# mLSTM decode state: sample-query products alternate between two column groups of PSUM, with a per-head add of the two partial sums

## The chip, the cores and the metric

The program runs on one core of one Trainium2 chip. The metric is the device time of one execution in microseconds (us); lower is better. The tensor engine (PE) multiplies a stationary operand, loaded into its array first, with a moving operand that streams through it, and writes to PSUM: 128 partitions, 8 banks of 512 fp32 columns each. VectorE (DVE), ScalarE (ACT), GpSimd (POOL) and the DMA queue fed by SyncE (SP) run beside it and are synchronised by semaphores.

## The reference, cut to what matters

One inference step of a two-layer model for a prompt of 256 tokens and 8 samples of 4 new tokens (32 sample tokens). The part that the change touches is the mLSTM of layer 1: 4 heads of width 512, each sample with an old state C0 of 512x512 per head.

```python
num = jnp.einsum('btsh,bshe->bthe', w_intra, vc) + w_inter[..., None] * jnp.einsum('bthd,bhde->bthe', qc, C)
den = jnp.sum(w_intra, axis=2) + w_inter * jnp.einsum('bthd,bhd->bth', qc, n)
h = num / jnp.maximum(jnp.abs(den), jnp.exp(-m_t))[..., None]
C_new = decay[..., None, None] * C + jnp.einsum('bshd,bshe->bhde', kw, vc)
```

For the samples, the second term of `num` is the product of each sample's 4 scaled queries with its own old state, and `C_new` is the decayed old state plus an outer product of the sample's keys and values. All of it is in fp32.

## The kernel before, in words

The kernel is one hand-ordered program per engine. The dense matrices are streamed as weights through two buffers of 2 MB; that part (lines 1582 to 1584 on PE) is not touched. The mLSTM stage stands between the dense steps IN_C and OUT_C, and during it the weight buffers serve as a ring of 8 slots (`cring`), each holding half of one sample's state for one head: 2 tiles of 128x512.

Loops: for each head h of 4, for each sample b of 8, for each half of the state. A state tile index e runs over 4, two to a half.

- PE, `old_state(h, b, half)` (line 1914): for its two tiles, a matmul with the scaled queries of sample b as the stationary operand (128 rows, 32 columns, zero outside the sample's own 4 columns) and the state tile as the moving operand, 512 columns wide. All 32 such products of a head, and one product of the head's own 32 tokens (line 1941), add up in `ps[0:NS, 2, :]`, that is partitions 0 to 31 of bank 2. An fp32 matmul of the program appears in the trace as two weight loads and two matmul passes.
- PE, `outer(h, b, half)` (line 1930): two matmuls of 96x128 by 96x512 (fp32r, one pass each) into banks 0 and 1. It waits for `c_new`: the two banks are used by every half, so the DVE must have taken the half before.
- DVE, `new_state(h, b, half)` (line 1385): two `scalar_tensor_tensor` of 128x512 that read banks 0 and 1 and update the slot; then SP stores the slot (line 558) and loads the one six items ahead (line 549).
- `chunk(h, b)`: other work of the head and of the next one, spread over b on all engines. PE: denominators and numerators at b=0, key sums at b=1, the prompt's own state (`outer(h, NB, half)`, line 1933) at b=2 and 3, next head's projections at b=4, 5 and 6, its rows and scores at b=7. The last head has nothing of the next head to do at b=4 to 7.

PE's order for one sample before is: `old_state` half 0, `outer` half 0, `old_state` half 1, `outer` half 1, `chunk`.

At the end of a head (`chunk`, b=7), ACT copies the sum out of PSUM into `hs[:, h]` (line 931), squares it (line 934) and, if there is a next head, runs its exponentials (lines 891 to 893). DVE writes `y1_lo` (line 1430) and then makes the next head's queries (`queries`, lines 1335 to 1345) and score weights (`weights`, lines 1360 and 1361). After the last head, DVE scales `hs` (lines 1450 to 1459), PE transposes it (line 1983), DVE combines it (lines 1463 to 1467), and only then do the steps of OUT_C start.

The column group of a 32-column product follows from its PSUM partitions. Elsewhere in the kernel, `sample_scores(b)` (lines 1667 and 1669, layer 0) writes sample b's attention scores to the 32 partitions `32*(b % 4)`, so its column group changes at each new b; 1667 writes two wide passes into each of two banks, 1669 a narrow product of the own keys.

Of the kernel before, what the change touches and what calls it, by code (L numbers as in the profile page):

```python
# [21 lines left out]
ALU = mybir.AluOpType  # L22
ACT = mybir.ActivationFunctionType
AX = mybir.AxisListType

P = 128
D = 1024
SEQ = 256
NB = 8
# [96 lines left out]
def program(nc, A, O):  # L126
    ctx = ExitStack()
    with ctx:
# [187 lines left out]
        def sem(name):  # L316
            sems[name] = ctx.enter_context(nc.semaphore(name))
            return sems[name]
# [103 lines left out]
        h_ready = sem("h_ready")  # L422
        h_sq = sem("h_sq")
        hs_psum = sem("hs_psum")
        hs_taken = sem("hs_taken")
        hs_sq = sem("hs_sq")
        hs_mean = sem("hs_mean")
# [35 lines left out]
        def item(h, b, half):  # L463
            return ITEMS * h + ORDER.index((b, half))

        def loads(i):

            return sum(1 for j in range(i % C_SLOTS, i + 1, C_SLOTS) if ORDER[j % ITEMS][0] < NB)
# [125 lines left out]
        def _(act):  # L594
# [310 lines left out]
            def chunk(h, b):  # L905
                if b == 0:
                    act.wait_ge(den_psum, h + 1)
                    act.activation(stok[:, 0, h:h + 1], ps[0:NS, 3, SEQ:SEQ + 1], ACT.Abs)
                    act.activation(dn, ps[:, 3, 0:SEQ], ACT.Abs).then_inc(den_abs, 1)
                if b == 1:  # L910
                    act.wait_ge(h_ready, h + 1)
                    act.activation(qf[:, :, 0:SEQ], hT, ACT.Square).then_inc(h_sq, 1)
                if b == 3:
                    act.activation(dn, staged(h, "mean")[:, 0:SEQ], ACT.Sqrt, bias=tiny[:, 0:1], scale=1.0 / DH
                                   ).then_inc(stage_read_a, 1)
                if b == 4 and h + 1 < NH:
                    qk(h + 1)
                if b == 5 and h + 1 < NH:
                    keys_by_token(h + 1)
                    own_keys(h + 1)  # L920
                if b == 6:
                    if h + 1 < NH:
                        values_by_token(h + 1)
                    act.wait_ge(y1_full, h + 1)
                    act.activation(y1_hi[:, ET * h:ET * h + ET, 0:SEQ], hT, ACT.Copy).then_inc(y1_hi_ready, 1)
                if b == 7:
                    if h + 1 < NH:
                        head_rows(h + 1)

                    act.wait_ge(hs_psum, h + 1)  # L930
                    act.activation(hs[:, h], ps[0:NS, 2, :], ACT.Copy).then_inc(hs_taken, 1)
                    act.wait_ge(hs_taken, h + 1)

                    act.activation(fold[0:NS].rearrange("p a b -> p (a b)")[:, 0:DH], hs[:, h], ACT.Square, accum_out=stok[:, 1, h:h + 1]).then_inc(hs_sq, 1)
                    if h + 1 < NH:
                        exps(h + 1)
# [29 lines left out]
        def _(dve):  # L966
# [428 lines left out]
            def chunk(h, b):  # L1395
                if b == 0:

                    dve.wait_ge(den_abs, h + 1)
                    order.after(dve.tensor_tensor(dn, dn, bc[:, h % 2, R_EN:R_EN + SEQ], ALU.max))
                    order.after(dve.reciprocal(dn, dn))  # L1400
                    dve.wait_ge(num_psum, h + 1)
                    dve.tensor_tensor(hT, ps[:, 4:6, :].rearrange("p a (c t) -> p (a c) t", t=SEQ),
                                      dn.unsqueeze(1).to_broadcast([P, ET, SEQ]), ALU.mult).then_inc(h_ready, 1)
                if b == 1:
                    new_n(h)
                if b == 2:
                    new_state(h, NB, 0)
                if b == 3:
                    new_state(h, NB, 1)
                if b == 4:  # L1410
                    dve.wait_ge(stage_read_a, reads(use(h, "mean"))[1])
                    order.after(dve.reciprocal(dn, dn))
                    for e in range(ET):
                        order.mark(dve.scalar_tensor_tensor(hT[:, e], hT[:, e], pcol("norm_w", ET * h + e), dn,
                                                            ALU.mult, ALU.mult))
                if b == 5:
                    order.wait()
                    for e in range(ET):
                        m = ET * h + e
                        order.mark(dve.scalar_tensor_tensor(hT[:, e], xcc[:, m, 0:SEQ], pcol("skip", m), hT[:, e],  # L1420
                                                            ALU.mult, ALU.add))
                    if h + 1 < NH:
                        keys_low(h + 1)
                    order.wait()
                    dve.tensor_tensor(hT, hT, z[:, ET * h:ET * h + ET, 0:SEQ], ALU.mult).then_inc(y1_full, 1)
                if b == 6 and h + 1 < NH:
                    values_low(h + 1)
                if b == 7:
                    dve.wait_ge(y1_hi_ready, h + 1)
                    dve.tensor_tensor(y1_lo[:, ET * h:ET * h + ET, 0:SEQ], hT, y1_hi[:, ET * h:ET * h + ET, 0:SEQ],  # L1430
                                      ALU.subtract).then_inc(y1_ready, 1)
                    if h + 1 < NH:
                        queries(h + 1)
                        arguments(h + 1)
                        weights(h + 1)
# [134 lines left out]
        def _(pe):  # L1570
# [330 lines left out]
                    last = pe.matmul(out[:, c0:c0 + NB], kst[:, h % 2, es], seln, start=True, stop=True)  # L1901
                last.then_inc(stage_full, 1)

            def old_state(h, b, half):

                i = item(h, b, half)
                s = i % C_SLOTS
                if h and b == half == 0:
                    pe.wait_ge(hs_taken, h)
                pe.wait_ge(qs_ready, h + 1)  # L1910
                pe.wait_ge(c_in[s], 16 * loads(i))
                for d in range(HD2):
                    e = HD2 * half + d
                    last = pe.matmul(ps[0:NS, 2, :], qz_of1(h, e, b), cring[:, s, d], start=b == e == 0,  # L1914
                                     stop=b == NB - 1 and e == ET - 1, skip_group_check=True)
                return last

            def outer(h, b, half):
# [17 lines left out]
            def chunk(h, b):  # L1936
                if b == 0:
                    denominators(h)
                    numerators(h)

                    pe.matmul(ps[0:NS, 2, :], ew[0:NS, 3 * P:3 * P + NS], vtk_s, start=False, stop=False,
                              skip_group_check=True)
                if b == 1:
                    key_sums(h)
# [23 lines left out]
            scores(0)  # L1968
            for h in range(NH):
                for b in range(NB):  # L1970
                    for half in range(2):
                        last = old_state(h, b, half)
                        if b == NB - 1 and half == 1:
                            last.then_inc(hs_psum, 1)
                        outer(h, b, half)
                    chunk(h, b)

# [133 lines left out]
```

## Time and profile before

| | us |
|---|---|
| median of 3 runs | 1517.96 |
| lowest, highest | 1515.53, 1520.9 |
| span of the profiled execution | 1518.3 |
| mLSTM stage in it (first `old_state` to last `outer`) | 922.25 to 1209.06 |

The profile gives the span of the profiled execution; it stands 0.3 us above the median. In its rows, PE is a matmul pass and PEld a weight load; a timeline row gives start, duration and the instructions merged into it, and in brackets the engine's idle time before it with what ended it. "x4" on line 1914 is two matmuls of the program. Matmul ends are modelled, so starts are the firmer number.

### The profile page before, as it was taken

The page shows a single profiled execution, that of the slowest core. Times are in us where ns is not written, and L with a number is a line of the kernel's source. Part 1 is how long each engine was busy: PE and PEld are TensorE (multiplying, and loading weights), DVE is VectorE, ACT ScalarE, POOL GpSimd, SP SyncE. Part 2 cuts the span into 40 slices and gives each one's busy share as a digit, 9 for nine tenths or more (in the row PEclk, how much of TensorE's full clock was granted, in tenths as well). Part 3 has the DMA queues.
Part 4 walks back from the last instruction along what each step waited for, and adds up shares of the span by engine and source line. Part 5 has one row for each costly group of instructions (what it writes and reads, how often), then busy time and mean ns, then how long its engine had stood idle before and what let it go on. Part 6 is the DMA issues. An engine that isn't in the chain of part 4 may idle for free.

```text
span 1518.3 us, 21716 instructions
## 1 busy us (share of the span) xinstructions
PE 1372.2 (90%) x8383; PEld 1101.8 (73%) x8383; DVE 705.4 (46%) x1032; ACT 526.1 (35%) x846; POOL 155.3 (10%) x244
## 2 busy tenths in 40 slices
PE   4999799879999799999799979999999787999995
PEld 4999233369989699999699945444444286999995
DVE  5545624521113654434657434555555645544343
ACT  5333022411113465433435243232332143555341
POOL 2000000000000222100360031010000002222000
PEclk9999699969989799999799799999999988999998
DMA  7444278738744154444244013767676853444340
GB/s 261 165 161 160 100 255 264 244 124 254 243 141 160 56 174 166 159 167 166 70 171 161 26 58 124 254 228 260 214 267 210 272 201 111 152 162 160 137 166 31
DMA packets 68587, 260.25 MB, mean 171 GB/s; under 512 B 7780, under 2 KB 9124, under 8 KB 60584
## 3 DMA queue, kind: packets, MB, share of 16 engines
q1 hardware_dynamic: 68520, 259.32, 49.2%
q8 instruction: 46, 0.75, 0.2%
q14 instruction: 21, 0.17, 0.0%
HBM read 217.57 MB, written 41.73 MB: 171 GB/s over the span
## 4 chain that ended last, share of the span: by engine, by line
PE 85%; DVE 8%; ACT 3%; issue 2%; DMA 2%; POOL 1%; SPq 0%; POOLq 0%; DVEq 0%; ACTq 0%
PE ps L1582 17%; PE ps L1584 16%; PE ps L1583 16%; PE ps L1914 7%; PE ps L1723 7%; PE ps L1667 4%; PE ps L1930 3%; PE ps L1933 2%; DVE x L1024 1%; PE ps L1819 1%; PE ps L1811 1%; PE ps L1624 1%; DMA kv<-in_kv 1%; PE ps L1643 1%; DVE cring L1385 1%
## 5 line engine op out<-in xcount | busy, mean ns | idle before, releaser
L1582 PE MATMUL ps<-xin_hi,w_hi 128*128 128x288 f32 x1088 | 335.6, 308 | 51.3 <-DVE xin_lo L1003 29.4
L973 DVE TENSOR_TENSOR w_lo<-w_raw,w_hi 128x1024 fp32r<-128x1024 f32 x232 | 282.8, 1222 | 199.7 <-ACT w_hi L605 199.3
L1583 PE MATMUL ps<-xin_lo,w_hi 128*128 128x288 f32 x1088 | 328.9, 302 | 0.0
L1584 PE MATMUL ps<-xin_hi,w_lo 128*128 128x288 f32 x1088 | 327.6, 301 | 0.0
L605 ACT ACTIVATE w_hi<-w_raw 128x1024 fp32r<-128x1024 f32 x232 | 243.0, 1055 | 236.0 <-PE ps L1584 223.2
L1582 PEld LDWEIGHTS ps<-xin_hi,w_hi 128*128 128x128 f32 x1088 | 211.2, 194 | 59.7 <-issue 40.5
L1583 PEld LDWEIGHTS ps<-xin_lo,w_hi 128*128 128x128 f32 x1088 | 212.5, 195 | 0.5
L1584 PEld LDWEIGHTS ps<-xin_hi,w_lo 128*128 128x128 f32 x1088 | 212.6, 195 | 0.0
L1582 PE MATMUL ps<-hid_hi,w_hi 128*128 128x288 f32 x512 | 153.1, 299 | 5.7 <-POOL hid_lo L1504 5.7
L1583 PE MATMUL ps<-hid_lo,w_hi 128*128 128x288 f32 x512 | 152.4, 298 | 0.0
L1584 PE MATMUL ps<-hid_hi,w_lo 128*128 128x288 f32 x512 | 152.0, 297 | 0.0
L1385 DVE SCALAR_TENSOR_TENSOR cring<-cring,bc,ps 128x512 f32<-128x512 f32 x128 | 90.0, 745 | 83.0 <-PE ps L1930 82.9
L1914 PE MATMUL ps<-cring,qz 128*32 128x512 f32 x256 | 121.8, 598 | 0.0
L1667 PE MATMUL ps<-kv,qz 128*32 128x448 f32 x256 | 103.5, 549 | 6.3 <-issue 4.3
L1723 PE MATMUL ps<-kv,pT 128*32 128x128 f32 x896 | 103.0, 277 | 0.0
L1723 PEld LDWEIGHTS ps<-kv,pT 128*32 128x32 f32 x896 | 98.0, 112 | 6.1 <-issue 5.3
L1582 PEld LDWEIGHTS ps<-hid_hi,w_hi 128*128 128x128 f32 x512 | 97.4, 190 | 6.1 <-issue 6.1
L1584 PEld LDWEIGHTS ps<-hid_hi,w_lo 128*128 128x128 f32 x512 | 97.7, 191 | 0.0
L1583 PEld LDWEIGHTS ps<-hid_lo,w_hi 128*128 128x128 f32 x512 | 97.4, 190 | 0.0
L1035 DVE SCALAR_TENSOR_TENSOR relu<-ps,rstd 128x288 f32<-128x288 f32 x64 | 29.3, 457 | 93.1 <-PE ps L1584 93.0
L1914 PEld LDWEIGHTS ps<-cring,qz 128*32 128x32 f32 x256 | 22.9, 109 | 63.5 <-issue 62.5
L1504 POOL TENSOR_TENSOR hid_lo<-relu,hid_hi 128x288 f32 x64 | 52.2, 815 | 156.3 <-ACT hid_hi L673 156.3
(343 smaller groups left out, 1680.8 us busy)
## 6 DMA issues: line engine op xcount, KB each, us to landing
w_raw<-in_weights SPq DMA_DIRECT2D x58, 2048.0 KB, 8.1
kv<-in_kv SPq DMA_DIRECT2D x128, 448.0 KB, 4.2
cring<-in_C SPq DMA_DIRECT2D x64, 512.0 KB, 4.8
out_Cs<-cring SPq DMA_DIRECT2D x64, 512.0 KB, 3.7
out_Cp<-cring SPq DMA_DIRECT2D x8, 512.0 KB, 3.0
x<-in_x SPq DMA_DIRECT2D x1, 1152.0 KB, 5.2
out_v<-gaqkv SPq DMA_DIRECT2D x1, 1152.0 KB, 4.2
out_k<-gaqkv SPq DMA_DIRECT2D x1, 1152.0 KB
```

Source lines behind the costliest of these rows:

```text
L605: act.activation(w_hi[:, l % UM], w_raw[:, u % 2, l % UM], ACT.Copy).then_inc(hi_ready, 1)
L973: dve.tensor_tensor(w_lo[:, l % UM], w_raw[:, u % 2, l % UM], w_hi[:, l % UM], ALU.subtract).then_inc(lo_ready, 1)
L1385: last = dve.scalar_tensor_tensor(cring[:, s, e], cring[:, s, e], bc[:, h % 2, R_DECAY + b:R_DECAY + b + 1], ps[:, e, :], ALU.mult, ALU.add)
L1504: pool.tensor_tensor(hid_lo[:, bass.ds(m, 1)].rearrange("p a t -> p (a t)"), relu2[:, l], hid_hi[:, bass.ds(m, 1)].rearrange("p a t -> p ( ...
L1582: pe.matmul(ps[:, j, 0:T], w_hi[:, j, ws], hi, start=start and kk == 0, stop=False)
L1583: pe.matmul(ps[:, j, 0:T], w_hi[:, j, ws], lo, start=False, stop=False)
L1584: last = pe.matmul(ps[:, j, 0:T], w_lo[:, j, ws], hi, start=False, stop=stop and kk == UK - 1)
L1667: pe.matmul(ps[part, 2 * f + c, 0:NK // 2], lhs, kv[:, s, c * NK // 2:(c + 1) * NK // 2], start=h == 0, stop=h == H - 1, skip_group_check= ...
L1723: last = pe.matmul(out, pT[:, kt, c0:c0 + 32], kv[:, s, P * kt:P * kt + P], start=False, stop=kt == KT - 1, skip_group_check=True)
L1914: last = pe.matmul(ps[0:NS, 2, :], qz_of1(h, e, b), cring[:, s, d], start=b == e == 0, stop=b == NB - 1 and e == ET - 1, skip_group_check= ...
L1930: last = pe.matmul(ps[:, d, :], kst[:, h % 2, es], vb[:, (NB * h + b) % 2], start=True, stop=True)
L1933: last = pe.matmul(ps[:, d, :], ktok[:, tt, es], vw[:, tt], start=tt == 0, stop=tt == 1)
```

## The change

Three things change together.

1. `old_state(h, b)` now does all four tiles of a sample in one run, ahead of both `outer` halves; it waits for both halves of the state to be loaded. PE's order for one sample becomes: `old_state` (4 matmuls), `outer` half 0, `outer` half 1, `chunk`.
2. Tile e goes to the group of 32 partitions `g = 2*(h % 2) + e % 2` of the same bank 2. Within a head the products alternate between two groups; even heads use partitions 0 to 63, odd heads 64 to 127. The head's own product goes to the first of the two. With two heads' sums apart, the wait for `hs_taken` reaches back two heads instead of one.
3. The two partial sums are added per head: ACT copies one (`hs_half`), DVE adds the other from PSUM to it (`hs_taken`), and ACT's square waits for that. The DVE instruction stands between `y1_lo` and the next head's queries.

```diff
@@ ACT, chunk b=7
                     act.wait_ge(hs_psum, h + 1)
-                    act.activation(hs[:, h], ps[0:NS, 2, :], ACT.Copy).then_inc(hs_taken, 1)
+                    g = NS * 2 * (h % 2)
+                    act.activation(hs[:, h], ps[g + NS:g + 2 * NS, 2, :], ACT.Copy).then_inc(hs_half, 1)
                     act.wait_ge(hs_taken, h + 1)
@@ DVE, chunk b=7
                                       ALU.subtract).then_inc(y1_ready, 1)
+                    g = NS * 2 * (h % 2)
+                    dve.wait_ge(hs_half, h + 1)
+                    dve.tensor_tensor(hs[:, h], ps[g:g + NS, 2, :], hs[:, h], ALU.add).then_inc(hs_taken, 1)
                     if h + 1 < NH:
                         queries(h + 1)
@@ PE
-            def old_state(h, b, half):
-
-                i = item(h, b, half)
-                s = i % C_SLOTS
-                if h and b == half == 0:
-                    pe.wait_ge(hs_taken, h)
+            def old_state(h, b):
+
+                if h >= 2 and b == 0:
+                    pe.wait_ge(hs_taken, h - 1)
                 pe.wait_ge(qs_ready, h + 1)
-                pe.wait_ge(c_in[s], 16 * loads(i))
-                for d in range(HD2):
-                    e = HD2 * half + d
-                    last = pe.matmul(ps[0:NS, 2, :], qz_of1(h, e, b), cring[:, s, d], start=b == e == 0,
-                                     stop=b == NB - 1 and e == ET - 1, skip_group_check=True)
+                for half in range(2):
+                    i = item(h, b, half)
+                    pe.wait_ge(c_in[i % C_SLOTS], 16 * loads(i))
+                for e in range(ET):
+                    g = 2 * (h % 2) + e % 2
+                    s = item(h, b, e // HD2) % C_SLOTS
+                    last = pe.matmul(ps[NS * g:NS * g + NS, 2, :], qz_of1(h, e, b), cring[:, s, e % HD2],
+                                     start=b == 0 and e < 2, stop=b == NB - 1 and e >= 2, skip_group_check=True)
                 return last
@@ PE, the loop
                 for b in range(NB):
+                    last = old_state(h, b)
+                    if b == NB - 1:
+                        last.then_inc(hs_psum, 1)
                     for half in range(2):
-                        last = old_state(h, b, half)
-                        if b == NB - 1 and half == 1:
-                            last.then_inc(hs_psum, 1)
                         outer(h, b, half)
                     chunk(h, b)
```

PE's order, last head, samples 4 and 5 (`c_in` is the load of a ring slot, `c_new` the DVE's update of the half before). Before:

```order
L1914 MATMUL ps<-cring,qz_149 32x512 [waits c_in2,qs_ready]
L1914 MATMUL ps<-cring,qz_149 32x512
L1930 MATMUL ps<-vb,kst 128x512 [waits vb_ready,stage_read_v,c_new]
L1930 MATMUL ps<-vb,kst 128x512
L1914 MATMUL ps<-cring,qz_149 32x512 [waits c_in3,qs_ready]
L1914 MATMUL ps<-cring,qz_149 32x512
L1930 MATMUL ps<-vb,kst 128x512 [waits vb_ready,stage_read_v,c_new]
L1930 MATMUL ps<-vb,kst 128x512
```

And now:

```order
L1920 MATMUL ps<-cring,qz_149 32x512 [waits c_in3,c_in2,qs_ready]
L1920 MATMUL ps<-cring,qz_149 32x512 x3
L1936 MATMUL ps<-vb,kst 128x512 [waits vb_ready,stage_read_v,c_new]
L1936 MATMUL ps<-vb,kst 128x512
L1936 MATMUL ps<-vb,kst 128x512 [waits vb_ready,stage_read_v,c_new]
L1936 MATMUL ps<-vb,kst 128x512
```

The two runs of two query products became one run of four, and nothing stands any more between the two outer products, the second of which waits for the DVE.

DVE's order at the end of the last head (`stok` are the per-token factors of the sample outputs). Before:

```order
L1385 SCALAR_TENSOR_TENSOR cring<-cring,bc,ps 128x512 [waits c_in7,c_mm]
L1385 SCALAR_TENSOR_TENSOR cring<-cring,bc,ps 128x512
L1430 TENSOR_TENSOR y_lo<-hT,y_hi 128x4x256 [waits y1_hi_ready]
L1450 TENSOR_TENSOR stok<-stok,tokg_s 32x4
L1451 RECIPROCAL stok<-stok 32x4 [waits v_order]
L1453 TENSOR_TENSOR stok<-stok 32x4 [waits hs_sq,v_order]
```

And now:

```order
L1387 SCALAR_TENSOR_TENSOR cring<-cring,bc,ps 128x512 [waits c_in7,c_mm]
L1387 SCALAR_TENSOR_TENSOR cring<-cring,bc,ps 128x512
L1432 TENSOR_TENSOR y_lo<-hT,y_hi 128x4x256 [waits y1_hi_ready]
L1436 TENSOR_TENSOR hs<-ps,hs 32x512 [waits hs_half]
L1455 TENSOR_TENSOR stok<-stok,tokg_s 32x4
L1456 RECIPROCAL stok<-stok 32x4 [waits v_order]
L1458 TENSOR_TENSOR stok<-stok 32x4 [waits hs_sq,v_order]
```

The add came in behind `y_lo`, and the wait for `hs_sq` (ACT's square) now hangs on it.

## Rows read from the trace of the kernel before

**Rows 1.** Engines in a stretch: from:to, length, busy (count) of each, PEclk, DMA share, GB/s.

```profile
922.00:1210.80 288.80, 268.82 (x973) 119.43 (x972) 156.23 (x268) 76.67 (x137) 4.34 (x12) 1.00 0.70 236
```

**Rows 2.** Timeline, head 2, sample 1: start us, us, engine, line.

```profile
1081.69 1.90 PE L1914 MATMUL ps<-cring,qz 128*32 128x512 f32 x4
...
1083.52 0.73 PE L1930 MATMUL ps<-vb,kst 96*128 96x512 f32 x2
...
1084.19 1.90 PE L1914 MATMUL ps<-cring,qz 128*32 128x512 f32 x4
1084.30 1.41 DVE L1385 SCALAR_TENSOR_TENSOR cring<-cring,bc,ps 128x512 f32<-128x512 f32 x2 [2.18 <-PE ps L1930]
...
1086.02 0.30 PEld L1930 LDWEIGHTS ps<-vb,kst 96*128 96x128 f32 x2 [0.84 <-DVE cring L1385]
```

**Rows 3.** Timeline, last head, sample 5, PE alone.

```profile
1196.94 0.73 PE L1930 MATMUL ps<-vb,kst 96*128 96x512 f32 x2 [1.85 <-DVE cring L1385]
```

**Rows 4.** Timeline, last head, samples 5 and 6, DVE alone.

```profile
1195.48 1.40 DVE L1385 SCALAR_TENSOR_TENSOR cring<-cring,bc,ps 128x512 f32<-128x512 f32 x2
1197.71 1.41 DVE L1385 SCALAR_TENSOR_TENSOR cring<-cring,bc,ps 128x512 f32<-128x512 f32 x2 [0.83 <-PE ps L1930]
...
1201.88 1.40 DVE L1385 SCALAR_TENSOR_TENSOR cring<-cring,bc,ps 128x512 f32<-128x512 f32 x2
```

**Rows 5.** Timeline, head 0, sample 6: DVE, then PE's loads.

```profile
981.66 1.41 DVE L1385 SCALAR_TENSOR_TENSOR cring<-cring,bc,ps 128x512 f32<-128x512 f32 x2
...
983.13 0.30 PEld L1930 LDWEIGHTS ps<-vb,kst 96*128 96x128 f32 x2 [0.84 <-DVE cring L1385]
```

**Rows 6.** Timeline of PE's matmuls: within sample 2 of `sample_scores`; from sample 3 to 4.

```profile
222.85 0.92 PE L1667 MATMUL ps<-kv,qz 128*32 128x448 f32 x2
...
236.77 0.75 PE L1667 MATMUL ps<-kv,qz 128*32 128x448 f32 x2
...
237.15 0.22 PE L1669 MATMUL ps<-gaqkv,qz 128*32 128x32 f32 x2
```

**Rows 7.** Timeline of PE's weight loads, `sample_scores`, from sample 3 to 4.

```profile
236.95 0.14 PEld L1667 LDWEIGHTS ps<-kv,qz 128*32 128x32 f32 x2
237.15 0.11 PEld L1669 LDWEIGHTS ps<-gaqkv,qz 128*32 128x32 f32 x1
```

**Rows 8.** View of line 1328: ns min/median/max, first and last start, forms.

```profile
L1328 DVE TENSOR_TENSOR vst<-ps,vst x4: 683/683/683, 916.4 to 1137.8; 32x512 fp32r<-32x512 f32 x4
```

**Rows 9.** Timeline, from head 1 to head 2.

```profile
1070.49 0.29 DVE L1345 TENSOR_TENSOR qn<-qn,par 128x128 f32<-128x128 f32 x1
...
1071.76 0.14 PEld L1914 LDWEIGHTS ps<-cring,qz 128*32 128x32 f32 x2
...
1072.96 0.17 DVE L1361 TENSOR_TENSOR ew<-ew,ps 32x32 f32<-32x32 f32 x1
...
1074.37 1.40 DVE L1385 SCALAR_TENSOR_TENSOR cring<-cring,bc,ps 128x512 f32<-128x512 f32 x2 [1.25 <-PE ps L1930]
```

**Rows 10.** Timeline, end of the stage and start of OUT_C.

```profile
1209.05 0.63 ACT L934 ACTIVATE fold<-hs 32x512 f32<-32x512 f32 x1
...
1209.59 0.18 ACT L934 ACTIVATION_READ_ACCUMULATOR fold<-hs 32x1 f32 x1
...
1211.55 0.14 DVE L1450 TENSOR_TENSOR stok<-stok,tokg_s 32x4 f32<-32x4 f32 x1
...
1211.93 0.15 DVE L1453 TENSOR_TENSOR stok<-stok 32x4 f32<-32x4 f32 x1
...
1220.90 0.60 PE L1582 MATMUL ps<-y_hi,w_hi 128*128 128x288 f32 x1 [5.39 <-DVE y_lo L1472]
```

**Rows 11.** Engines in stretches, columns as in the first group.

```profile
626.20:629.10 2.90, 0.06 (x2) 0.06 (x1) 0.84 (x2) 2.25 (x4) 0.80 (x1) 1.00 0.00 0
...
630.60:633.80 3.20, 3.20 (x16) 3.20 (x15) 0.48 (x1) 0.00 (x0) 0.00 (x0) 0.50 0.54 113
...
1192.00:1204.00 12.00, 8.82 (x23) 2.27 (x21) 10.38 (x17) 1.78 (x2) 0.00 (x0) 1.00 0.64 225
```

More of the change, by code:

```diff
@@ L424, in program @@
         hs_psum = sem("hs_psum")
+        hs_half = sem("hs_half")
         hs_taken = sem("hs_taken")
@@ L1939, in chunk @@
                     numerators(h)
-                    pe.matmul(ps[0:NS, 2, :], ew[0:NS, 3 * P:3 * P + NS], vtk_s, start=False, stop=False,
+                    g = NS * 2 * (h % 2)
+                    pe.matmul(ps[g:g + NS, 2, :], ew[0:NS, 3 * P:3 * P + NS], vtk_s, start=False, stop=False,
                               skip_group_check=True)
```

## Prediction

> **What bounds the kernel now.** I read the stretches first, to find which part of the span the change touches, then the timeline of the mLSTM stage, then the places where its pattern breaks. Everything outside the stage from 922 to 1221 us keeps its instructions, so the sum is made over this stage. In it the tensor clock is granted in full and PE shows 268.82 of 288.80 us busy [rows 1], but a busy PE says little here: the modelled ends of four query passes cover their own draining. The timeline says more. For one half of a state, the query products start at 1081.69, the outer products at 1083.52 (1.83 us later), the next query products at 1084.19 (0.67 later), and the next outer products at 1086.02 (1.83 later) [rows 2]. So a half takes 2.50 us from outer product to outer product. The DVE starts on the two banks 0.78 us after the outer products begin and needs 1.41 us, until 1085.71, while PE comes for the banks at 1086.02 [rows 2]: between two halves of one sample PE is last by 0.31 us, though the bracket names the DVE. This pattern, 2.50 us from half 0 to half 1, stands in 27 of the 32 sample steps (4 heads by 8 samples).
>
> It breaks in five. In samples 5 and 6 of the last head the DVE, busy with the head's output, comes late: PE stood idle 1.85 us for it [rows 3]. There DVE ends at 1196.88 (1195.48 + 1.40) and PE goes on at 1196.94, 0.06 us later, and the DVE starts again 0.77 us after that, at 1197.71 [rows 3, 4]. In sample 6 of heads 0 to 2 the DVE is the limit too: it ends at 983.07 and the outer products follow at 983.13 [rows 5].
>
> **The change part by part.**
>
> *Between the halves.* Nothing stands any more between the two outer products of a sample, so the second follows the first as fast as the DVE lets it: 0.77 us until the DVE starts, 1.41 us of DVE, 0.06 us until PE goes on [rows 2 to 4], 2.24 us in place of 2.50. That is 0.26 us less in each of the 27 steps. In the other five the DVE already set the time and its own chain doesn't shrink: nothing. The total for this part is 27 x 0.26 = 7.0 us less. The price of the part is cover: the 1.90 us of query products that ran beside the DVE in this gap [rows 2] now run ahead of the first outer products, where the next paragraph counts them.
>
> *The run of four query products.* It lies on PE's path from one sample to the next. Before, half of it did: 1.83 us from its first pass to the outer products, four passes 0.43 us apart (a matmul of the program is two passes; 1.90 us for four, of which the last takes some 0.6 us to its modelled end, leaves 1.3 us for three steps) [rows 2]. Now it is eight passes, A A B B A A B B in program order, where A and B are the two column groups. Does the array run A and B side by side? The trace of before doesn't show this run, but it shows a change of column group in `sample_scores`. Two wide passes of one group take 0.92 us together, so the second starts 0.38 after the first [rows 6]. At the change from partitions 96 to 127 to partitions 0 to 31, two wide passes take 0.75 us together, from 236.77 [rows 6]: the new group's pass starts some 0.21 us after the old group's wide pass, inside it. And the old group's two narrow passes, which come earlier in the program, start at 237.15, 0.38 us after their own group's last pass [rows 6]: neither stream slowed the other. Even the order is not kept: the new group's weights are loaded at 236.95, ahead of the old group's at 237.15 [rows 7]. So a pass that waits for its own group lets one of the other group by. If that holds in the run, A and B go side by side with four steps as before, B behind A by the time in which its two predecessors are loaded, some 0.03 us each (two loads merge into 0.14 us where one takes 0.11 [rows 7]). I take 1.89 us for the whole run, 0.06 more than 1.83. This estimate's bounds are 1.83 (no lag) and 1.83 + 4 x 0.43 = 3.55 (no overlap at all). I take the lower end because the row at 236.77 is the same kind of pass, fp32 with 32 columns, and I keep the other for the rivals; one difference is that there the two groups wrote to different banks, and here both write to bank 2. Cost: 27 x 0.06 = 1.6 us. In sample 6 of heads 0 to 2 the DVE hides it (it starts 0.26 us later than PE's outer products would allow), and in samples 5 and 6 of the last head it stands behind the wait of 1.85 us [rows 3].
>
> One page weighs against this. The Trainium skill, TensorE: Matmul & The Clock Gate, section "Part 3: Packing small matmuls — row/col tiling", says that matmuls of different tiles overlap, but start and end strictly in program order. By that rule the run would take five steps, the sum would be the first rival's, and the rows at 236.95 and 237.15 disagree with it.
>
> *The add, heads 0 to 2.* DVE gets one instruction of 32x512 with a PSUM operand; line 1328 has that shape and takes 0.68 us [rows 8]. It stands ahead of the next head's queries, which end at 1070.78 where PE first loads them at 1071.76 [rows 9]: 0.98 us of slack for 0.68. Behind ACT's wait for the add are the square, the load of the exponential table, the exponentials, and the copy for sample 1; the DVE's `weights` end at 1073.13 and its next work starts at 1074.37 [rows 9], 1.24 us of slack for a shift of at most 0.9. So I cost these three at nothing. Were the cover gone, they would cost 0.7 to 0.9 each, 2 to 3 us.
>
> *The add, last head.* Here nothing hides it. Before, ACT's square was done at 1209.77, long before DVE came to line 1453 at 1211.93 [rows 10]. Now the add starts where line 1450 did, at 1211.55, ends at 1212.23, the square and its read-out take 0.72 us (1209.05 to 1209.77) [rows 10], and with 0.05 us for two semaphores line 1453 starts at about 1213.0: 1.1 us later. OUT_C starts on the DVE's last piece of this chain [rows 10], so all of it counts.
>
> *Waits that move.* Both halves of a state must have landed before its first product. PE waited for no load in the stage, and loads are issued six items ahead, three samples of 5 us at least. No cost. The wait for `hs_taken` goes back a head; it wasn't late before. No gain. Drains of the array between 32-column and 128-column work are halved in number, but those that go were beside the DVE's work and are in the 2.24 us.
>
> *The clock.* PE will be idle about 1.5 us in each step, as it is today at b=2 and 3, with a full clock. But in sample 5 of the last head the gap of 1.85 us grows by the 1.9 us of products that move out of it, to some 3.7 us, and in sample 6 to 3.2. Such a gap was followed by a lower clock elsewhere: PE did almost nothing from 626.20 to 629.10 and ran at 0.50, the 1.2 GHz level, from 630.60 to 633.80 [rows 11]; in 1192 to 1204 it is 1.00 today [rows 11]. Three microseconds at half rate slow a run of four steps by 1.7 us. If they fall on sample 6 the DVE hides most of it, if on sample 7 nothing does. Bounds 0 and about 4 us (two such runs and their outer products); I take 0.5.
>
> *Sum.* -7.0 + 1.6 + 0 + 1.1 + 0.5 = -3.8 us. The profiled span is 1518.3, the median 1518.0, so the two stand for each other: 1518.0 - 3.8 = 1514.2 us.
>
> **The rivals.**
>
> *Strict order (slower).* If a pass can't go ahead of one that waits, A A B B A A B B overlaps only where the group changes: A2 with B1, B2 with A1 and so on. Eight passes then take five steps in place of four: 0.43 us more per run, against 0.26 gained between the halves. Both count in 30 steps now, since the DVE has no slack left in those three of [rows 5] either: 30 x 0.17 = 5.1, plus 1.1 and 0.5, gives 6.7 us more, 1524.7 us. It decides against the change once the run takes more than about 2.0 us (0.26 less the 1.6 us of the ends spread over 27 steps is 0.2 us above 1.83). For it: program order is the simple case. Against it: rows 6 and 7. Chance 10%.
>
> *No overlap in one bank.* If two groups that write to the same bank take turns, the change doesn't do what it says: eight steps, 1.71 us more per run, less 0.26, in 30 steps 43.5, plus 1.6: 45 us more, 1563 us. For it: no row shows two groups in one bank. Against it: a product of full width writes all 128 partitions of one bank at once. Chance 7%.
>
> *The clock falls in earnest.* The 4 us above in place of 0.5: 1517.7 us, which is no change. Chance 10%.
>
> *More than reckoned.* No lag in the run and no clock loss: -7.0 + 1.1 = -5.9, 1512.1 us. It is the near end of my own case.
>
> **How the numbers follow.** My case has 73%, the other three 27%. A measurement of this kernel can tell about 0.3%, 4.6 us, from no change. My case lies between 1512 and 1516, and three runs of one kernel lay 5 us apart, so it falls on both sides of 1513.4: I put 40 of its 73 below (faster) and 33 above (no change). No change gets the clock's 10 less 2 for a worse end, 41 in all. Slower gets 10 + 7 + 2 = 19. The range takes in my case with the spread of the runs and strict order: 1509 to 1525.
>
> **What would show it.** In the trace of after: from the first query pass to the outer products 1.9 us (2.3 for strict order, 3.5 for none); passes of a run starting in pairs 0.06 us apart; 2.24 us between the two outer products; the add of 0.68 us at four places with PE's first product of a head not waiting for it; 1.1 us more from the last update of the state to OUT_C; PEclk of the last head's stretch. I am wrong if the run takes over 2.0 us, if the second outer products come later than 2.3 us after the first, or if a wait for a load or for the queries appears in front of the run.

## The result: 2.6% slower, and the profile after

| | kernel before | kernel after |
|---|---|---|
| median of 4 runs | 1516.74 us (1513.92 to 1520.9) | 1556.26 us (1552.38 to 1560.01) |
| ratio to before, 95% interval | 1 | 1.0256 (1.0226 to 1.0286) |
| span of the profiled execution | 1518.3 us | 1551.2 us |
| stage, first query product to last outer product | 286.4 us | 321.1 us |
| granted clock over the stage | 1.00 | 0.85 |

The forecast was 1514.2 us, and its range ended at 1525. The profiled execution of after is 32.9 us longer, and the stage alone is 34.7 us longer, so what happened, happened there.

The stage as a whole and four stretches of head 2 (columns as in [rows 1]: from:to, length, busy and count of PE, PEld, DVE, ACT, POOL, then PEclk, DMA share, GB/s):

```profile
919.10:1240.20 321.10, 255.61 (x968) 130.57 (x967) 156.62 (x268) 75.22 (x133) 4.33 (x12) 0.85 0.62 210
1093.60:1097.00 3.40, 3.40 (x13) 2.96 (x12) 2.18 (x2) 0.75 (x2) 0.00 (x0) 0.50 0.72 222
1097.00:1103.80 6.80, 5.30 (x25) 2.30 (x23) 2.93 (x4) 1.30 (x2) 0.00 (x0) 1.00 0.16 60
1103.90:1110.60 6.70, 6.70 (x25) 3.68 (x24) 1.45 (x5) 0.38 (x1) 0.00 (x0) 0.50 0.68 219
1110.70:1114.00 3.30, 1.36 (x4) 0.49 (x4) 1.81 (x3) 0.34 (x1) 0.00 (x0) 1.00 0.09 35
```

Before, PEclk was 1.00 here and PE modelled as busy for 268.82 of 288.80 us [rows 1]; now PE is busy 255.61 of 321.10 us and the clock swings between its two levels, 2.4 GHz (1.00) and 1.2 GHz (0.50). The trace has 20 pieces at 0.50 in this stage. The page shows the same in its row of granted clocks over 40 slices of the span, where the stage lies in slices 24 to 32:

```profile
PEclk9999699889989799999897978879797879899998
```

The timeline of PE over one step at full clock and the next one mostly at half clock (start, length, engine, line, operation, count of passes, in brackets the idle time ahead and what ended it; a program's matmul is two passes):

```profile
1098.66 1.91 PE L1920 MATMUL ps<-cring,qz 128*32 128x512 f32 x8
1100.50 0.73 PE L1936 MATMUL ps<-vb,kst 96*128 96x512 f32 x2
1102.73 0.73 PE L1936 MATMUL ps<-vb,kst 96*128 96x512 f32 x2 [1.50 <-DVE cring L1387]
...
1107.01 3.63 PE L1920 MATMUL ps<-cring,qz 128*32 128x512 f32 x8
1110.57 0.76 PE L1936 MATMUL ps<-vb,kst 96*128 96x512 f32 x2
1112.83 0.73 PE L1936 MATMUL ps<-vb,kst 96*128 96x512 f32 x2 [1.50 <-DVE cring L1387]
```

At full clock all is as the sum had it: eight passes at L1920 are through in 1100.50 - 1098.66 = 1.84 us, no more than four of them took before (1.83) [rows 2], and the second outer products follow the first after 1102.73 - 1100.50 = 2.23 us. At half clock the same run takes 1110.57 - 1107.01 = 3.56 us. Nothing but the clock differs between the two.

That the two column groups really run side by side shows in the weight loads, same step, PEld:

```profile
1098.65 0.14 PEld L1920 LDWEIGHTS ps<-cring,qz 128*32 128x32 f32 x4 [0.84 <-issue]
...
1099.11 0.12 PEld L1920 LDWEIGHTS ps<-cring,qz 128*32 128x32 f32 x2 [0.31 <-issue]
...
1099.54 0.12 PEld L1920 LDWEIGHTS ps<-cring,qz 128*32 128x32 f32 x2 [0.31 <-issue]
```

The eight loads come as four, two and two, 0.43 to 0.46 us apart. With all products in one group (e1_one_group below) they come as two and then six single ones, 0.43 us apart. The rows don't name the group; that a bunch of two is one load for each group is read from the program's order.

The view of waits for PE, over the stage (engine, line, waited for: us in total, times, longest). After:

```profile
PE ps L1936 <- DVE cring L1387: 50.9, 32, 3.7
PE ps L1939 <- DVE cring L1387: 12.0, 8, 1.5
```

and before, the same two places:

```profile
PE ps L1933 <- DVE cring L1385: 12.0, 8, 1.5
PE ps L1930 <- DVE cring L1385: 3.2, 2, 1.9
```

PE stood idle beside the DVE in 2 of 32 steps before; now it does in all 32, for 50.9 us in all. The page gives the query products 121.8 us busy before and 68.9 now. So two things were taken out of the stage together: the work that covered the DVE, and about half of the time in which PE streams query products.

### The profile page after: what moved, and what is told of

Read it like the earlier page. It is cut to its first block, busy times and chain, and to the rows that moved or that the text cites. A ratio compares the mean times of both kernels' runs of the same rounds, so it can differ in the third digit from the quotient of the medians.

```text
span 1551.2 us, 21690 instructions
## 1 busy us (share of the span) xinstructions
PE 1355.2 (87%) x8383; PEld 1107.9 (71%) x8383; DVE 708.2 (46%) x1036; ACT 526.5 (34%) x846; POOL 154.9 (10%) x244
## 4 chain that ended last, share of the span: by engine, by line
PE 81%; DVE 9%; ACT 3%; issue 3%; DMA 2%; POOL 1%; SPq 0%; POOLq 0%; DVEq 0%; ACTq 0%
PE ps L1587 16%; PE ps L1589 16%; PE ps L1588 16%; PE ps L1728 6%; PE ps L1672 4%; PE ps L1920 4%; PE ps L1939 3%; PE ps L1936 3%; DVE cring L1387 2%; PE ps L1824 1%; PE ps L1864 1%; DMA kv<-in_kv 1%; DVE x L1026 1%; PE ps L1816 1%; PE ps L1629 1%
## 5 line engine op out<-in xcount | busy, mean ns | idle before, releaser
L1936 PE MATMUL ps<-vb,kst 96*128 96x512 f32 x128 | 48.5, 461 | 50.9 <-DVE cring L1387 50.9
L1936 PEld LDWEIGHTS ps<-vb,kst 96*128 96x128 f32 x128 | 19.7, 194 | 96.1 <-DVE cring L1387 67.1
L1920 PE MATMUL ps<-cring,qz 128*32 128x512 f32 x256 | 68.9, 663 | 0.0
```

Source lines behind the costliest of these rows:

```text
L1920: last = pe.matmul(ps[NS * g:NS * g + NS, 2, :], qz_of1(h, e, b), cring[:, s, e % HD2], start=b == 0 and e < 2, stop=b == NB - 1 and e >= ...
L1936: last = pe.matmul(ps[:, d, :], kst[:, h % 2, es], vb[:, (NB * h + b) % 2], start=True, stop=True)
```

## Experiments

The two clock levels say what the time went on, not why the level fell. A prediction that counts on "1.5 us idle is harmless" needs to know. The theories:

- **A, share of work**: the clock falls when PE streams for too little of the time, by whatever cause. The change took both 1.5 us of cover in each step and some 50 us of streaming out.
- **B, the hole**: the idle 1.5 us between the two outer products in each step does it.
- **C, two streams at once**: two column groups running together do it.
- **D, both**: holes and thinned-out passes each take from the clock, and add up. It is A with the holes and the passes told apart.
- **E, thrown-away work doesn't count**: fill matmuls wouldn't hold the clock, so a kernel with fills tells nothing.

Time at half clock is worked out from the windows: 2 x (1 - PEclk) x length, so 2 x 0.15 x 321.1 = 96 us for after. PEclk has two digits, so these figures are good to some 3 us. Stage and PEclk are those of the one profiled execution. The mean clock over the whole execution is known of every run, and it was 0.904 to 0.908 in the four of after and 0.934 to 0.944 in those of before. The first four experiments were timed beside the same runs of before (median 1517.01 us of 8), the last four beside others (1518.35 us of 19). The ratio is taken from the runs round by round, so it can differ from the quotient of the medians, by 0.2% for e3_split and 0.3% for e4_half_products.

| kernel | median us | ratio, 95% | stage us | PEclk | at half clock, us |
|---|---|---|---|---|---|
| after | 1556.26 | 1.0256 (1.0226 to 1.0286) | 321.1 | 0.85 | 96 |
| e1_one_group | 1597.8 | 1.0521 (1.0497 to 1.0546) | 368.2 | 0.89 | 81 |
| e2_fill | 1527.14 | 1.0061 (1.0038 to 1.0084) | 293.9 | 0.94 | 35 |
| e3_split | 1507.25 | 0.9916 (0.9885 to 0.9946) | 278.5 | 0.90 | 56 |
| e4_half_products | 1507.59 | 0.991 (0.9879 to 0.994) | 278.6 | 0.89 | 61 |
| e5_split_fill | 1498.91 | 0.9875 (0.9847 to 0.9904) | 266.6 | 0.97 | 16 |
| e6_fill4 | 1519.67 | 1.0005 (0.9989 to 1.0021) | 288.5 | 0.99 | 6 |
| e7_after_all_filled | 1518.51 | 0.9999 (0.9979 to 1.0019) | 291.7 | 0.95 | 29 |
| e8_split_fill_some | 1502.78 | 0.9899 (0.9877 to 0.9922) | 269.1 | 0.95 | 27 |

### e1_one_group: the new order without the second column group

```
-                    g = 2 * (h % 2) + e % 2
+                    g = 2 * (h % 2)
```

(ACT copies that one group, the DVE's add becomes an operation of the same size on `hs` alone, and the `start` and `stop` flags follow the one sum.)

> The order of the changed kernel (four products in one run, then both outer products), but all products in one group of 32 partitions; the DVE instruction stays as an in-place maximum of hs with itself, so the per-head chain is as long. Theory A (the tensor clock falls because the engine streams for too small a part of the time, overlapped products counting once): nothing overlaps, the engine streams as long as before, the granted clock stays at 1.00 in the mLSTM stage, the run takes 3.55 us, time about 1517 + 44 = 1561 us. Theory B (it falls because of the hole of 1.5 us between the two outer products of every step): the hole is there, the clock falls as in the changed kernel, 1580 us or more. Theory C (it falls because two groups stream at once): clock stays, 1561 us.

Measured: 1597.8 us. Window of the stage, and one step of PE's timeline at full clock:

```profile
917.10:1285.30 368.20, 305.14 (x968) 143.90 (x965) 156.31 (x268) 75.66 (x135) 4.32 (x12) 0.89 0.55 185
```

```profile
966.97 3.62 PE L1920 MATMUL ps<-cring,qz 128*32 128x512 f32 x8
970.52 0.73 PE L1936 MATMUL ps<-vb,kst 96*128 96x512 f32 x2
972.75 0.73 PE L1936 MATMUL ps<-vb,kst 96*128 96x512 f32 x2 [1.50 <-DVE cring L1387]
```

With one group the eight passes take 970.52 - 966.97 = 3.55 us at full clock, so the second group is worth 3.55 - 1.84 = 1.71 us a step: this is what the change was to bring, and it does. The clock falls without any overlap too (0.89), so the overlap isn't needed for a fall, and C alone can't carry the result. B had 1580 us or more. PE is modelled as busy for 305.14 of 368.20 us, 83%, against 80% in after: the hole of 1.50 us is the same in both. That is what B says; but after has 15 us more at half clock in a stage 47 us shorter, so the hole isn't all of it. A had 1561 us and a clock of 1.00 for this kernel and missed by 37 us: it had reckoned with as much streaming as before, but not with the longer step, of which that is a smaller share.

### e2_fill: a matmul without use in the hole

```
                     outer(h, b, 0)
+                    fill(h, 1)
                     outer(h, b, 1)
```

`fill` multiplies `ones` by `par[:, 0:512]` into 32 partitions of the other head's group in bank 2; nobody reads it.

> The changed kernel plus one fp32 matmul of 128x32 by 128x512 (two passes) between the two outer products of each step, into the two-group area of the other head that nobody reads; its result is thrown away. It should end 1.65 us after the first outer product starts, before the DVE is done at 2.24, and cost nothing in itself. Theory A: the clock stays at 1.00 for most of the stage, time 1512 to 1525 us. Theory B: the hole is filled, the same. Theory C: the clock falls as before or more, 1550 us or more.

Measured: 1527.14 us, 29 us less than after, by adding work, and 2 us above the range that A and B had for it. The hole, in PE's timeline (fill, then the second outer products):

```profile
963.65 1.04 PE L1946 MATMUL ps<-par,ones 128*32 128x512 f32 x2
...
965.23 0.73 PE L1936 MATMUL ps<-vb,kst 96*128 96x512 f32 x2 [0.53 <-DVE cring L1387]
```

```profile
918.30:1212.20 293.90, 258.71 (x1036) 118.56 (x1033) 156.33 (x268) 76.10 (x135) 4.33 (x12) 0.94 0.68 230
```

Two passes of 0.43 us turn a hole of 1.50 us into one of 0.53, and the time at half clock falls from 96 to 35 us. E is refuted: useless streaming holds the clock. It also shows that the slow time in after is the clock's, since no wait, no load and no dependence has been taken out.

### e3_split: two column groups in the old order

```
+            def old_state(h, b, half):
...
+                for d in range(HD2):
+                    e = HD2 * half + d
+                    g = 2 * (h % 2) + d % 2
```

The query products of each half stand ahead of that half's outer products again, as before; each half's two products go to the two groups.

> Two groups, but the order of the kernel before (products of half 0, outer product 0, products of half 1, outer product 1). Each half's two products overlap: 0.98 us from their start to the outer product in place of 1.83, so a step loses 0.26 between the halves and 0.85 ahead of the first: 30 x 0.85 + 27 x 0.26 = 32 us at full clock, 1486 us. The hole beside the DVE is 0.6 us. Theory A: streaming time per step is as small as in the changed kernel and the step shorter; the clock falls in parts of the stage, some 15 to 30 us are lost of the 32: 1500 to 1520 us. Theory B: no long hole, clock 1.00, 1486 us. Theory C: clock falls as in the changed kernel, 1515 us or more.

Measured: 1507.25 us, ratio 0.9916, faster than both kernels. One step of PE's timeline, in sample 6, and the stage:

```profile
973.68 1.05 PE L1920 MATMUL ps<-cring,qz 128*32 128x512 f32 x4
974.66 0.73 PE L1936 MATMUL ps<-vb,kst 96*128 96x512 f32 x2
975.32 1.05 PE L1920 MATMUL ps<-cring,qz 128*32 128x512 f32 x4
978.00 0.73 PE L1936 MATMUL ps<-vb,kst 96*128 96x512 f32 x2 [1.63 <-DVE cring L1387]
```

```profile
922.30:1200.80 278.50, 240.17 (x971) 115.26 (x969) 156.23 (x268) 75.99 (x135) 4.33 (x12) 0.90 0.72 243
```

Four passes now take 974.66 - 973.68 = 0.98 us where they took 1.83 [rows 2]. The second products stand beside the DVE, so most steps have a hole of some 0.5 us only (this one, where the DVE's other work comes between, has 1.63); the clock is still 0.90, where B had 1.00 and 1486 us. So the hole of 1.5 us in every step isn't needed for a fall. But not all holes are small here. The view of waits for PE over the stage has the eight at b = 2 and 3 as before, and one of 3.0 us:

```profile
PE ps L1936 <- DVE cring L1387: 22.1, 29, 3.0
PE ps L1939 <- DVE cring L1387: 12.0, 8, 1.5
```

e8_split_fill_some below takes the long ones out. The gain expected at full clock was some 6 us too high as well, an estimate: the stage of e5_split_fill, 266.6 us with 16 of them at half clock, would be some 260 at full clock, and the expectation had 286.4 - 32 = 254. In samples 3, 6 and 7 of heads 0 to 2 the DVE is last, not PE, and what PE saves there is waited away.

### e4_half_products: half of the products, one group

```
-                for d in range(HD2):
+                for d in range(1):
```

This is an edit of before, and the `stop` flag follows it. It leaves out half of the samples' old-state products.

> The kernel before with one of the two query products of each half left out (half of the old-state products of the samples are missing from the output). The engine's timetable is that of e3_split, with no two passes at once. Theory A: the same time and clock as e3_split. Theory B and theory C: clock 1.00, 1485 us; if e3_split is slower than this one at a lower clock, two streams at once cost clock by themselves.

Measured: 1507.59 us, ratio 0.991.

```profile
965.61 0.72 PE L1930 MATMUL ps<-vb,kst 96*128 96x512 f32 x2 [0.52 <-DVE cring L1385]
...
968.96 1.04 PE L1914 MATMUL ps<-cring,qz 128*32 128x512 f32 x2
969.94 0.73 PE L1930 MATMUL ps<-vb,kst 96*128 96x512 f32 x2
970.60 1.04 PE L1914 MATMUL ps<-cring,qz 128*32 128x512 f32 x2
```

```profile
917.70:1196.30 278.60, 241.19 (x843) 116.15 (x840) 154.49 (x265) 75.54 (x135) 4.34 (x12) 0.89 0.72 243
```

This is the cleanest pair of the study. e3_split runs four passes in two streams, e4_half_products two passes in one stream; on PE's time line they take the same 1.0 us, and the two kernels agree in time (1507.25 and 1507.59), stage (278.5 and 278.6) and clock (0.90 and 0.89; over whole executions 0.916 to 0.927 and 0.919 to 0.929). The overlap as such costs nothing that these runs can tell, which spread over 10 us each: C is refuted as the cause of the loss. What counts is for how long PE streams, not how much it does meanwhile.

### e6_fill4: four passes of fill in the hole

`fill(h, 2)` in place of `fill(h, 1)` of e2_fill.

> The changed kernel with two thrown-away matmuls (four passes) between the outer products of each step, as many as the kernel before has of real ones there. The step between the halves goes back to 2.50 us. Theory D: apart from the last head's two waits the engine streams at least as long as before; clock 1.00 nearly everywhere, 1518 to 1522 us. Theory E: 1550 us or more.

Measured: 1519.67 us, ratio 1.0005.

```profile
1063.99 1.91 PE L1920 MATMUL ps<-cring,qz 128*32 128x512 f32 x8
1065.83 0.73 PE L1936 MATMUL ps<-vb,kst 96*128 96x512 f32 x2
1066.49 1.90 PE L1946 MATMUL ps<-par,ones 128*32 128x512 f32 x4
1068.33 0.73 PE L1936 MATMUL ps<-vb,kst 96*128 96x512 f32 x2
```

```profile
922.50:1211.00 288.50, 271.60 (x1097) 120.36 (x1095) 156.32 (x268) 75.26 (x133) 4.34 (x12) 0.99 0.69 234
```

Here everything of the change is in place, and PE's occupation is about what it was before (271.60 of 288.50 us here, 268.82 of 288.80 in [rows 1]): four passes ahead of the second outer products (1068.33 - 1065.83 = 2.50 us, the old distance [rows 2]) and a run of 1.84 us ahead of the first. Time and clock are those of before within the spread (0.99 and 1.00, some 6 us at half clock). The eight holes of 1.5 us at b = 2 and 3 are still there, 12.0 us in all, and one of 1.9 us. So the groups, the run of eight, the added operation on the DVE and the moved waits together cost nothing that the times can tell (the operation's 1.3 us at the end, below, is within the spread); what after lost hangs on what stood in the hole.

### e7_after_all_filled: every hole of after filled, none lengthened

After each first outer product a fill of 512 and one of 192 columns (in samples 5 and 6 of the last head four and three of 512, where the hole is longer); the same before the outer products of `NB` at b = 2 and 3.

> The changed kernel with all its waits filled as in e5_split_fill. Theory D: the clock holds, and the sum of the prediction without its clock term is met: 1517 - 4.3 = 1513 us. Theory E: 1550 us or more.

Measured: 1518.51 us, ratio 0.9999. That is 38 us less than after and some 5 us above the 1513 expected.

```profile
916.80:1208.50 291.70, 280.17 (x1135) 129.21 (x1133) 156.35 (x268) 76.08 (x135) 4.33 (x12) 0.95 0.68 232
```

29 us at half clock remained, though PE is modelled as busy for 280.17 of 291.70 us (96%). In before it was 93% [rows 1] with a clock of 1.00. So the busy share of the profile is not what the clock follows. The remaining falls come back at like places of heads 0 to 2 (at 986.9, 1065.4 and 1140.5 us, and again some 20 us later). What PE does ahead of those places is the small matmuls of the key sums and of a head's end, but no run took these alone. e6_fill4 has the same matmuls there and no fall. It has more idle time, 13.9 us of waits for the DVE against 8.4 here, but four passes of 512 columns as fill in each step, where this kernel has two of 512 and two of 192. So idle time alone doesn't order the two. What differs between them is the thinner fill, and the filled holes at b = 2 and 3 and in the last head; no run changed the fill by itself, and why the falls come at just these places stays open.

### e5_split_fill and e8_split_fill_some: how much the clock still holds in the split order

e5_split_fill is e3_split with fills of 512 and 192 columns ahead of each second outer product and of the outer products of `NB`; e8_split_fill_some keeps only those at b = 2 and 3 and in the last head:

```
                         last = old_state(h, b, half)
...
+                        if half and h == NH - 1 and b in (5, 6):
+                            fill(h, *((512,) * (4 if b == 5 else 3)))
                         outer(h, b, half)
```

> e3_split with thrown-away matmuls (128x32 by up to 512 columns, the other head's groups of bank 2) in every place where the tensor engine waits for the DVE: 512 and 192 columns beside the second half's products of each step and ahead of the prompt state's outer products at b=2 and 3, four and three of 512 in samples 5 and 6 of the last head. They fit in the waits by the rows (0.67 + 1.55 is 2.22 of 2.24 us). Theory D (the clock falls where waits and sparse passes together leave the engine too little to do; both the hole and the overlap count, the concurrency itself not): clock 1.00 in nearly all of the stage, about 1517 - 30 = 1487 us. Theory E (work that is thrown away in the same small groups doesn't hold the clock, and e2_fill gained by chance): 1505 us as e3_split.

> e5_split_fill without the filling of the ordinary step: only the waits of 1.5 us at b=2 and 3 and those of the last head are filled. Theory D: between e3_split and e5_split_fill, nearer to which tells whether the many short waits or the few long ones cost the clock; 1492 to 1502 us. A theory by which only long idle stretches count gives the time of e5_split_fill, 1487 us.

Measured: 1498.91 us (0.9875) and 1502.78 us (0.9899).

```profile
918.20:1184.80 266.60, 248.71 (x1135) 120.78 (x1132) 156.37 (x268) 75.97 (x135) 4.33 (x12) 0.97 0.74 253
```

```profile
913.20:1182.30 269.10, 242.86 (x1016) 115.18 (x1014) 156.25 (x268) 75.99 (x135) 4.33 (x12) 0.95 0.74 251
```

Filling the holes of e3_split takes 40 of its 56 us at half clock away and 278.5 - 266.6 = 11.9 us off the stage; the few fills of e8_split_fill_some bring most of it (9.4 us). So in this order the few long holes cost most of the clock, and the many short ones the smaller part (27 us at half clock were left with them, 16 without). Their medians lie 3.9 us apart and their intervals overlap, so which of the two is better isn't told, and a theory by which only the long holes count isn't excluded by these times. D missed both numbers: e5_split_fill came 12 us above its 1487, at 0.97, and e8_split_fill_some 0.8 us above its range. By time the intervals of e5_split_fill and e3_split overlap a little; the clock over the whole execution parts them, 0.930 to 0.933 in all runs against 0.916 to 0.927. Both beat before and after, e5_split_fill by 1.25% over before, at the price of matmuls whose results are thrown away. The version without such work, e3_split, gives 0.84%.

### What stands

| theory | verdict | by |
|---|---|---|
| C, overlap lowers the clock | refuted | e3_split and e4_half_products alike |
| B, the hole of 1.5 us in every step alone | refuted | e3_split and e4_half_products lose 0.10 with holes of some 0.5 us in most steps; e8_split_fill_some loses 0.05 with the long ones filled |
| E, fills don't hold the clock | refuted | e2_fill, e6_fill4, e7_after_all_filled |
| A, share of work, by the modelled busy share | refuted as a measure | e7_after_all_filled: 96% busy at 0.95, before: 93% at 1.00 |
| D, holes and thinned streaming together | agrees in direction with all eight | e6_fill4 restores streaming beside the DVE, and with it the time |

D says which way, not how much: its numbers were met by e6_fill4 and missed by e5_split_fill (12 us), e7_after_all_filled (5 us) and e8_split_fill_some (0.8 us), and the remaining falls of e7_after_all_filled aren't derived from it. A counted by real streaming, without the modelled ends, was not tested and is hardly told from D.

The price follows from two kernels that differ in fills alone. After and e7_after_all_filled have the same chain at full clock (2.23 us between outer products, runs of 1.84 us). If the fills cost e7 nothing, (321.1 - 291.7) / (96 - 29) = 0.44 us of stage were lost per microsecond at half clock; half the clock can't lose more than 0.5. The same from all their runs, with the mean clock over the whole execution, is 38 us for 93 at half clock, 0.41. Between e3_split and e5_split_fill it is 11.9 / 40 = 0.30, so the price isn't one number: where PE waits for the DVE anyway, a slower PE is likely to cost less, which no run took alone. After at full clock would be 321.1 - 0.44 x 96 = 279 us long. The terms of the prediction for the stage, 286.4 - 7.0 + 1.6 less what the run didn't cost (1.3), give 279.7. The two meet, and leave some 42 us for the clock, an estimate good to a few us.

## Why the prediction was wrong, point by point

- **Between the halves, 27 x 0.26 us: right.** The second outer products follow after 2.23 us (2.24 said) in 24 of the 27 steps, and after 2.26 to 2.72 us in the three that a half clock touches; in sample 6 of heads 0 to 2 the DVE sets 2.48 us (2.50 before).
- **The run, 1.89 us: right, slightly high.** It takes 1.84 us; the second group lags by nothing that can be seen. The term was +0.3 us, not +1.6. This settled the two dear rivals: strict order would have taken 2.3 us and no overlap 3.5. The reason given, that a pass waiting for its own group lets one of the other by [rows 6, 7], holds within one bank too.
- **The add, heads 0 to 2: right, nothing.** PE's first product of a head doesn't wait for it. The DVE waited for ACT's copy there, up to 0.8 us, which I had not named; e6_fill4, with the same waits, has the time of before.
- **The add, last head, 1.1 us: right, 0.2 low.** From the last outer products to OUT_C's first matmul it is 12.23 us before and 13.64 after; e4_half_products with the old chain has 12.46, e2_fill, e5_split_fill and e6_fill4 about 13.5, e3_split 13.75. That is 1.1 to 1.4 from start to start. Counted from the modelled end of the last outer product, which takes out the clock of that product, it is 11.84 us in both kernels without the add and 13.12 to 13.17 in those with it: 1.3 us. The chain itself, in the timeline of after:

```profile
1243.37 0.69 DVE L1436 TENSOR_TENSOR hs<-ps,hs 32x512 f32<-32x512 f32 x1
...
1244.09 0.63 ACT L936 ACTIVATE fold<-hs 32x512 f32<-32x512 f32 x1 [5.71 <-DVE hs L1436]
...
1244.92 0.15 DVE L1458 TENSOR_TENSOR stok<-stok 32x4 f32<-32x4 f32 x1 [0.59 <-ACT fold L936]
```

- **Waits that move: right, nothing.** No wait for a load stands ahead of the run.
- **The clock, 0.5 us with bounds 0 and 4: wrong, some 42 us (the estimate above).** This is the step that failed. It began with "PE will be idle about 1.5 us in each step, as it is today at b=2 and 3, with a full clock", and from there priced the clock only where a gap grew beyond that, in samples 5 and 6 of the last head. That gap did come (3.7 us, in the view of waits) and so did a half clock behind it, from 1226.7 to 1233.5; but it was one piece of 20. The precedent didn't carry, though the holes themselves were harmless: e6_fill4 has them at b = 2 and 3 too, and a clock of 0.99. The reason is in the company they had: at b = 2 and 3 a hole of 1.5 us stood twice a head among steps that streamed 1.83 us ahead of each outer product and beside the DVE. Those neighbours were what the change took out. The bound was then drawn from the two longest gaps, and the one rival that reached so far, no overlap in one bank, rested on another mechanism; a rival "the clock falls all through the stage" stood nowhere, though [rows 11] showed what a fall looks like.

What I should have seen: the gain of the change, some 50 us less of streaming, is a loss of PE's occupation wherever something else sets the pace. The DVE set it here: 2.23 us from outer to outer whatever PE does. A step lost 1.90 us of 5 us of PE's work to save 0.26 us.

The Trainium skill, TensorE: Matmul & The Clock Gate, section "HAM oscillation — how this bites in real kernels", tells of a matmul kernel that falls to the lower clock in every round because PE waits for DMA between groups of matmuls. The waits that it tells of are some 3 to 5 us long. The pieces at 0.50 here show the same back and forth, but with waits for the DVE of mostly 1.5 us, and e7_after_all_filled fell six times with waits for the DVE of 0.2 to 0.5 us.

## What to carry to other kernels

Before packing small matmuls or moving PE work out of another engine's shadow, see what PE will then be doing there: where the DVE sets the pace, PE's saved time turns into idle time, and if the stage loses its clock each microsecond at the lower level costs up to half a microsecond (0.30 to 0.44 here). A hole that is harmless once in a while is no precedent for the same hole in every step. Packing paid off here only in the order that kept PE's products beside the DVE (e3_split, 0.84%), and of a stage where the clock is 1.00 one should ask how much PE work will be left in it once the change has taken out what it promises.

## What the runs showed of the hardware

- Passes of two column groups that write to the same PSUM bank run side by side, in program order A A B B A A B B too: eight fp32 passes of 512 columns take 1.84 us, as long as four of one group, and 3.55 us if all are of one group. The Trainium skill, TensorE: Matmul & The Clock Gate, section "Part 3: Packing small matmuls — row/col tiling", has matmuls start and end strictly in program order; by that the run would have taken one step of 0.43 us more, 2.3 us, and the trace disagrees.
- Two streams side by side hold the clock no better than one: e3_split and e4_half_products were granted 0.90 and 0.89.
- A stage modelled as 96% busy was granted 0.95 (e7_after_all_filled) and one at 93% was granted 1.00 (before), so PE's busy row alone doesn't tell whether the clock will hold.
- Matmuls whose result nobody reads made the kernel faster: 1556.26 us without, 1527.14 with two passes in each step, 1518.51 with the holes full.
